# Two expert layers: first pass's rows by one-hot products, place table inside the loop, gate rows by ScalarE's queue, two blocks' residual adds on GpSimd

## The chip, the cores and the metric

One core of a Trainium2 chip runs the whole program. The metric is the device time of one execution in microseconds (us). The engines are called PE (TensorE, the matrix products), DVE (VectorE), ACT (ScalarE), POOL (GpSimd) and SP (SyncE, which here only issues transfers).

## The reference, cut to what matters

Two layers run over 384 tokens of 1024 channels (128 context tokens, 256 latent tokens): a mixer (layer 0) or attention (layer 1), and after each a mixture of 32 experts:

```python
g_prob = softmax(x @ w_rg + b_rg)                 # 4 groups, the best one is taken
e_v, e_i = top_k(logits of that group's 8 experts, 2)
gate = softmax(e_v) * g_p                         # two experts and two gates per token
hid = silu(x @ w_g[e]) * (x @ w_u[e])             # 1024 -> 256
y = sum over the token's two experts of gate * (hid @ w_d[e])
x = x + m[5] * y                                  # m[5]: the layer's gate row (adaLN)
```

The next layer, or the end of the program, begins with an RMS norm of x. Everything is float32.

## The kernel before, in words

Tokens lie in three blocks of 128 partitions (`X`, `H`, `NB` = 3). The experts are paired (16 pairs). One **round** of the expert loop has 22 **passes**: the 6 heaviest pairs get two passes, the other 10 one; a pass takes up to 32 tokens of each expert of its pair (`SLOTS`). The number of rounds comes from the counts of tokens at run time. With these inputs it is one round in each layer, 44 passes in all.

Ahead of the loop (`experts(l)`, one function for each engine) the **routing** is computed: PE multiplies the normed rows by the router's weights, DVE picks the experts, PE counts tokens in front of each (L988), and DVE turns the counts into a slot (`slot_p`) and a place (`slot_c`, which pass) for each of a token's two experts. From these DVE builds one-hot operands, and PE sums them into tables: four columns first (L999, the rows of passes 0 to 3, turned into row numbers on DVE, L1843 to L1846), and then a table for all rounds at once (L1005, 2 x 136 columns, operands L1848 to L1850, results L1864 to L1869).

In a **pass** POOL fetches the pass's 64 rows from DRAM by an indirect transfer (`gather`, L622 the row numbers, L625 the transfer); PE turns them (`turn_rows`, L1013), ACT copies the turned rows to SBUF (`x_copy`, L1392), PE multiplies by the gate and up weights (L1058), ACT applies Silu (L1404), DVE multiplies (`HID`, L1913), PE turns (L1070) and multiplies by the down weights (L1080). ACT and DVE split the result in two parts (L1411, L1923), and in the next pass PE spreads them over the tokens by a one-hot product (`combine`, L1024); DVE adds that to the sums (`add_half`, L1886). The transfers of rows for passes 0 and 1 are issued before the loop, and each later one when PE has turned the rows two passes earlier.

The expert weights come by SP's queue: 2 MB for each of gate, up and down of a pair (L453), into a ring of six slots, so that two pairs are in SBUF. Six transfers are issued as the slots come free ahead of the loop; in the loop a pair's gate and up slots are loaded again when its last gate and up product is done (ACT counts `gate_up_used`), its down slot when its last down product is.

Also ahead of the loop of layer 0, PE computes rows of the modulation for later layers from weights that stand in those ring slots. The last of them is called `places`: products (L751), a sum (L767 to L769), ACT's copy (L1242, L1243), POOL's product with the gain (L571) and its store to DRAM (`mod_rows`, L561). SP loads the sixth expert chunk only when that store has landed. POOL's queue then loads the layer's gate rows (1 MB) and in layer 0 the next norm's shift and scale rows (2 MB, both L525) from `mod_rows`.

After the loop DVE does the **end**: it adds the last sums, multiplies by the gate rows (`update_block`, L1939), adds to `X` (L1940), and norms the block (`norm_block`; ACT gives the squares and the root): block 0, then 1, then 2. After layer 1 that norm (L1517) is the result, and POOL's queue stores it (L679).

## Time and profile before

| | |
|---|---|
| time, median of 3 runs | 1055.38 us (1053.33 to 1055.83) |
| the profiled execution: its time, its span | 1052.37 us, 1050.5 us |
| busy: PE, DVE, ACT, POOL | 878.1, 520.7, 206.9, 123.2 us |
| mean granted clock of PE | 0.91 of 2.4 GHz |
| moved by DMA | 304.67 MB, mean 290 GB/s |

Rows of a timeline give start and length in us, the engine, the line of the kernel, the operation and its tiles, and in brackets how long the engine had been idle and what ended that. "SPq" is a transfer issued by SP. Two full levels of PE's clock occur: 1.00 (2.4 GHz) and 0.50 (1.2 GHz).

### The profile page before, as it was taken

The numbers are of one execution on the slowest core, as the hardware profiler recorded it, in microseconds if no ns is written. First come the engines' busy times: TensorE is split into PE (matmuls) and PEld (weight loads), VectorE is DVE, ScalarE is ACT, GpSimd is POOL, SyncE is SP. The second block draws the span as 40 slices with busy tenths as digits, with TensorE's granted clock in tenths as the row PEclk, the third lists the DMA queues.
The fourth block names the chain that finished last, engine by engine and source line by source line (L and its number), as shares of the span: only waits on it lengthen the run. The fifth ranks groups of instructions, "written<-read, shape, count | busy, mean of one in ns | idle before, by whom it ended". The sixth has DMA issues, their size and how long they took to land.

```text
span 1050.5 us, 17780 instructions
## 1 busy us (share of the span) xinstructions
PE 878.1 (84%) x6776; PEld 475.1 (45%) x6776; DVE 520.7 (50%) x1257; ACT 206.9 (20%) x428; POOL 123.2 (12%) x196
## 2 busy tenths in 40 slices
PE   2799999999799899786687997899589979886850
PEld 0455454645355455443333465445455545443420
DVE  1257532244656555452445464524656646454354
ACT  2223141212111111110122115212011111111021
POOL 2300011300321010010001000020211101000000
PEclk9899999898899999898888999999599989898875
DMA  9992440938899999999998523021699999999921
GB/s 306 366 333 80 144 176 15 395 128 301 330 365 407 417 416 417 413 413 418 416 387 330 180 81 130 1 86 44 255 366 391 417 412 418 418 415 419 417 117 60
DMA packets 78198, 304.67 MB, mean 290 GB/s; under 512 B 11512, under 2 KB 11824, under 8 KB 52648
## 3 DMA queue, kind: packets, MB, share of 16 engines
q1 hardware_dynamic: 66072, 277.08, 66.9%
q0 software_dynamic: 10768, 21.78, 5.9%
q10 hardware_dynamic: 1280, 4.72, 1.1%
q8 instruction: 55, 0.90, 0.4%
q14 instruction: 23, 0.19, 0.0%
HBM read 317.10 MB, written 5.32 MB: 307 GB/s over the span
## 4 chain that ended last, share of the span: by engine, by line
PE 67%; DMA 13%; DVE 7%; issue 5%; SPq 3%; ACT 3%; DVEq 0%; POOL 0%; ACTq 0%
PE psum L727 16%; PE psum L1058 15%; DMA ring<-in_w_exp_up 9%; PE psum L1080 6%; PE psum L1024 5%; PE psum L799 4%; PE psum L925 4%; PE psum L1013 3%; PE psum L751 3%; DVE ht L1886 3%; SPq L448 2%; DMA ring<-in_w_in_odd 2%; DMA ring<-in_w_mod 2%; PE psum L973 1%; PE psum L1189 1%
## 5 line engine op out<-in xcount | busy, mean ns | idle before, releaser
L1058 PE MATMUL psum<-ring,arena 128*32 128x256 f32 x2816 | 193.6, 436 | 60.6 <-issue 41.7
L1886 DVE TENSOR_TENSOR ht<-ht,psum 128x512 f32<-128x512 f32 x276 | 172.8, 679 | 34.0 <-PE psum L1024 34.0
L1058 PEld LDWEIGHTS psum<-ring,arena 128*32 128x32 f32 x2816 | 107.1, 125 | 159.5 <-issue 100.7
L727 PE MATMUL psum<-ring,ht 128*128 128x512 f32 (+1 forms) x432 | 170.3, 551 | 3.4 <-ACT ht L1257 2.7
L727 PEld LDWEIGHTS psum<-ring,ht 128*128 128x128 f32 x432 | 81.4, 191 | 85.7 <-issue 77.1
L1024 PE MATMUL psum<-y_top,to_token 64*128 64x512 f32 x276 | 88.0, 468 | 14.5 <-DVE y_low L1923 4.0
L1913 DVE TENSOR_TENSOR arena<-arena,psum 64x256 f32<-64x256 f32 x44 | 18.1, 412 | 164.5 <-ACT arena L1404 164.5
L1080 PE MATMUL psum<-ring,arena 128*32 128x512 f32 x704 | 84.7, 598 | 0.0
L1024 PE MATMUL psum<-y_low,to_token 64*128 64x512 f32 x276 | 71.3, 417 | 0.0
L751 PE MATMUL psum<-ring,cond_silu 128*32 128x512 f32 x384 | 50.8, 669 | 21.1 <-DMA ring<-in_w_mod 21.1
L1411 ACT ACTIVATE y_top<-psum,arena 128x512 fp32r<-128x512 f32 x44 | 30.2, 687 | 181.6 <-PE psum L1080 181.6
L1404 ACT ACTIVATE arena<-psum 64x256 f32<-64x256 f32 x44 | 16.7, 380 | 217.0 <-PE psum L1058 217.0
L622 POOL CAST arena<-arena 128x1 uint32 (+1 forms) x48 | 10.1, 211 | 390.8 <-PE psum L1013 369.8
L1013 PEld LDWEIGHTS psum<-ident,arena 32*128 32x128 f32 x736 | 44.0, 197 | 22.9 <-issue 22.9
L625 POOL DMA_INDIRECT arena<-h_rows,arena x48 | 48.7, 1016 | 42.9 <-POOL arena L622 40.4
L1024 PEld LDWEIGHTS psum<-y_top,to_token 64*128 64x128 f32 x276 | 34.5, 185 | 41.9 <-DVE ht L1886 32.3
L1923 DVE SCALAR_TENSOR_TENSOR y_low<-psum,arena,y_top 128x512 fp32r<-128x512 f32 x44 | 33.0, 750 | 40.0 <-ACT y_top L1411 40.0
L1013 PE MATMUL psum<-ident,arena 32*128 32x32 f32 x736 | 49.1, 272 | 3.9 <-issue 3.9
L561 POOL DMA_DIRECT2D mod_rows<-ring x20 | 10.7, 539 | 285.1 <-ACT ring L1245 283.9
L799 PE MATMUL psum<-ht,ring 128*128 128x384 f32 x128 | 43.6, 497 | 0.0
L925 PE MATMUL psum<-ring,ht 128*128 128x512 f32 x96 | 42.4, 598 | 0.0
L1392 ACT COPY arena<-psum 128x512 f32<-128x512 f32 x46 | 27.0, 587 | 56.1 <-PE psum L1013 56.1
(329 smaller groups left out, 914.3 us busy)
## 6 DMA issues: line engine op xcount, KB each, us to landing
ring<-in_w_exp_gate SPq DMA_DIRECT2D x32, 2048.0 KB, 15.6
ring<-in_w_exp_up SPq DMA_DIRECT2D x32, 2048.0 KB, 20.8
ring<-in_w_exp_down SPq DMA_DIRECT2D x32, 2048.0 KB, 20.8
ring<-in_w_mod SPq DMA_DIRECT2D x24, 2048.0 KB, 17.2
ring<-in_w_in_even SPq DMA_DIRECT2D x5, 2048.0 KB, 19.7
shift_scale<-mod_rows POOLq DMA_DIRECT2D x3, 2048.0 KB, 10.7
ring<-in_w_in_odd SPq DMA_DIRECT2D x3, 2048.0 KB, 19.7
ring<-in_w_out_even SPq DMA_DIRECT2D x2, 2048.0 KB, 8.3
```

The costliest lines, as they stand in the source:

```text
L625: pool.indirect_dma_start(XS[v], None, h_rows[l], bass.IndirectOffsetOnAxis(ap=from_row[v][:, 0:1].bitcast(U32), axis=0), bounds_check=T - ...
L727: mm = pe.matmul(psum[:, to, 0:cols], HT[:, b, k, :], w[:, k, :], start=(k == 0), stop=(k == KC - 1))
L751: mm = pe.matmul(psum[32 * j:32 * j + 32, to, :], cond_silu[:, k, 2 - 2 * half:34 - 2 * half], w[:, k, :], start=(half == 0 and r == 0), s ...
L799: mm = pe.matmul(psum[:, to, 0:T], w[:, k, c * P:(c + 1) * P], HT[:, :, k, :], start=(k == 0), stop=(k == KC - 1))
L925: mm = pe.matmul(bank(OUT_BANKS[0][c]), HT[:, b, k, :], w[n][:, k, :], start=(k == 4), stop=(k == 3))
L1013: t = pe.transpose(psum[:, n, SLOTS * k:SLOTS * (k + 1)], XS[v][side, k:D:KC], ident[side, side])
L1024: mm = pe.matmul(bank(BACK_BANKS[2 * b + n]), to_token[v][side, b * P:(b + 1) * P], rows[side, :], start=(part == 0), stop=(part == 1))
L1058: mm = pe.matmul(psum[to:to + SLOTS, 2, 0:256], XT[:, e, k, :], RG[:, 3 * u + a, e, k, :], start=(k == 0), stop=(k == KC - 1))
L1080: mm = pe.matmul(psum[to:to + SLOTS, 4, :], HTS[v][:, k, SLOTS * e:SLOTS * (e + 1)], RD[:, 3 * u + 2, e, k, n * 512:(n + 1) * 512], start= ...
L1411: act.activation(Y_HI, bank(4), ACT.Copy, scale=token[v][:, 1:2]).then_inc(M("y_top"), 1)
L1886: dve.tensor_tensor(acc, acc, bank(BACK_BANKS[c]), ALU.add).then_inc(M("added"), 1)
L1923: dve.scalar_tensor_tensor(Y_LO, bank(4), token[v][:, 1:2], Y_HI, ALU.mult, ALU.subtract).then_inc(M("y_low"), 1)
```

## The change

1. **First pass's rows by products** (`first_rows`). DVE builds `first_hot`, which says for each token whether and in which slot it is in pass 0; PE multiplies the normed rows, which are still in `H`, by it: 24 products of 128x128 by 64 columns, which give pass 0's turned rows directly. The transfer of pass 0's rows and its `turn_rows` go. The small table has two columns (passes 1 and 2) instead of four; it stands between the two halves of the 24.
2. **The table inside the loop.** It has 25 columns for one round instead of 136 for six (`PLACES`). PE makes it in pass 0 after the gate and up products, DVE turns it into row numbers after `HID` of pass 0 (`table`), and only then may PE go on with that pass's `combine`. At the end of a round DVE lowers `slot_c` by 22 and builds the operands for the next one. POOL's loop is written out in 22 passes with fixed columns. The gates of the tokens and the number of rounds are computed earlier on DVE.
3. **Gate rows by ScalarE's queue.** ACT issues the loads of gate rows (and in layer 0 of shift and scale rows) ahead of the loop, after waiting for the last `mod_rows` store (`rest_stored`).
4. **Residual adds on GpSimd.** For blocks 1 and 2 DVE adds the sums and multiplies by the gate rows in PSUM (`gated_sum`), and POOL adds to `X`. Block 1's part comes before block 0's norm.

On PE ahead of layer 0's loop stood (L999 the small table, L767 to L769 the sum of `places`, L1005 the large table, L1013 the turn of pass 0's rows):

```order
L999 MATMUL psum<-arena 128x4 [waits routing_sb]
L999 MATMUL psum<-arena 128x4 x5
L767 MATMUL psum<-mod_bias,pick_bias 4x512 [waits rest_row_ready,mod_part_sb]
L768 MATMUL psum<-ring,pick 4x512
L769 MATMUL psum<-mod_bias,pick_bias 4x512
L1005 MATMUL psum<-arena 128x272 [waits routing_sb]
L1005 MATMUL psum<-arena 128x272 x5
L1013 MATMUL psum<-ident,arena 128x32 [waits rest_row_ready,moe0_gathered_0]
L1013 MATMUL psum<-ident,arena 128x32 x15
```

and now (L1002 is `first_rows`, L1010 the small table):

```order
L1002 MATMUL psum<-arena,h 128x64 [waits routing_sb,rest_row_ready]
L1002 MATMUL psum<-arena,h 128x64 x11
L1010 MATMUL psum<-arena 128x2 [waits routing_sb]
L1010 MATMUL psum<-arena 128x2 x5
L1002 MATMUL psum<-arena,h 128x64 x12
L766 MATMUL psum<-mod_bias,pick_bias 4x512 [waits rest_row_ready,mod_part_sb]
L767 MATMUL psum<-ring,pick 4x512
L768 MATMUL psum<-mod_bias,pick_bias 4x512
```

The wait for pass 0's rows (`moe0_gathered_0`) is gone, and the large table, now 128x50, follows the gate and up products of pass 0.

On ACT in the same place stood (L1235 to L1243 the copies of `places`, L1392 `x_copy`, L424 the number of rounds, after which the loop begins):

```order
L1235 COPY ring<-psum 128x512 [waits mod_part_ps]
L1242 COPY ring<-psum 4x512 [waits mod_sum_ps]
L1243 ACTIVATE ring<-psum 4x512
L1392 COPY arena<-psum 128x512 [waits moe0_x_ps]
L424 TENSOR_LOAD arena [waits rounds_ready]
```

and now:

```order
L1247 COPY ring<-psum 128x512 [waits mod_part_ps]
L1432 COPY arena<-psum 128x512 [waits moe0_x_ps]
L1254 COPY ring<-psum 4x512 [waits mod_sum_ps]
L1255 ACTIVATE ring<-psum 4x512
L1404 DMA gate_rows<-mod_rows 128x2048 [waits rest_stored]
L1404 DMA shift_scale<-mod_rows 128x4096
L426 TENSOR_LOAD arena [waits rounds_ready]
```

Between `x_copy` and the loop ACT now waits for the store of the `places` rows.

On DVE at the end of layer 1 stood, from block 0's gate rows on:

```order
L1939 TENSOR_TENSOR arena<-ht,gate_rows 128x512 [waits moe1_added]
L1940 TENSOR_TENSOR x<-x,arena 128x512 [waits dve_links]
L1939 TENSOR_TENSOR arena<-ht,gate_rows 128x512
L1940 TENSOR_TENSOR x<-x,arena 128x512 [waits dve_links]
L1884 REGISTER_ALU
L1886 TENSOR_TENSOR ht<-ht,psum 128x512 [waits moe1_back_ps]
L1884 REGISTER_ALU
L1886 TENSOR_TENSOR ht<-ht,psum 128x512 [waits moe1_back_ps]
L1501 SCALAR_TENSOR_TENSOR small<-small 128x1 [waits squares]
```

and now:

```order
L1984 TENSOR_TENSOR x<-x,arena 128x512 [waits dve_links]
L1991 REGISTER_ALU
L1992 TENSOR_TENSOR psum<-ht,psum 128x512 [waits moe1_back_ps]
L1994 TENSOR_TENSOR arena<-psum,gate_rows 128x512 [waits x_updated,dve_links]
L1991 REGISTER_ALU
L1992 TENSOR_TENSOR psum<-ht,psum 128x512 [waits moe1_back_ps]
L1994 TENSOR_TENSOR arena<-psum,gate_rows 128x512 [waits x_updated,dve_links]
L1526 SCALAR_TENSOR_TENSOR small<-small 128x1 [waits squares]
```

Block 1's two gate products come ahead of block 0's norm, and its additions to `X` are POOL's.

The diff's core:

```diff
-PLACES = MAX_ROUNDS * PASSES + 4
+PLACES = PASSES + 3
...
             # POOL
-                for q in range(2):
-                    gather(q, q, static=True)
+                for q in range(1, 3):
+                    gather(q, one(first_row[:, q - 1:q]), q % 2)
...
-                for v in range(2):
-                    one_pass(v, v, static=True)
-                load_rows(u, (2, 3), gt_t[:, :], "gate_in")
-                if l == 0:
-                    load_rows(2, (0, 2), gs_t[:, :], "rows_in")
-                pool.wait_ge(S("table_ready"), 2 * l + 2)
                 R = rounds_of(pool, l)
-                with pool.Fori(1, R * (PASSES // 2)) as i:
-                    for v in range(2):
-                        one_pass(i * 2 + v, v)
+                with pool.Fori(0, R) as r:
+                    pool.wait_ge(M("table"), r + 1)
+                    for p in range(PASSES):
+                        q = r * PASSES + p
+                        pool.wait_ge(M("x_ps"), q + 2)
+                        gather(q + 3, tab[:, 1:2, p + 3:p + 4], (p + 1) % 2)
...
+                for c in range(2, 6):
+                    b, n = divmod(c, 2)
+                    pool.wait_ge(M("added"), last * 6 + (13 + c))
+                    pool.tensor_tensor(X[:, b, cols], X[:, b, cols], UPD_M[n], ALU.add).then_inc(S("x_updated"), 1)
...
             # PE
+                def first_rows(some):
+                    for k in some:
+                        for b in range(NB):
+                            mm = pe.matmul(psum[:, X_BANKS[0], 2 * SLOTS * k:2 * SLOTS * (k + 1)], H[:, b, k:D:KC], first_hot[:, b, :],
+                                           start=(b == 0), stop=(b == NB - 1))
...
+                    if p == 0:
+                        pe.wait_ge(M("in_table"), r * 7 + 1)
+                        for i in range(6):
+                            mm = pe.matmul(psum[:, 7, 0:2 * PLACES], in_slot[:, i, :], in_pair[:, i], start=(i == 0), stop=(i == 5))
+                        mm.then_inc(M("table_ps"), 1)
                     turn_rows(q + 1, 1 - v)
                     if p == 0:
-                        pe.wait_ge(S("table_ready"), 2 * l + 2)
+                        pe.wait_ge(M("table"), r + 1)
...
             # ACT
-                x_copy(0)
+                act.wait_ge(M("x_ps"), 1)
+                act.copy(XT, bank(X_BANKS[0]).rearrange("p (k e s) -> p e k s", e=2, k=KC)).then_inc(M("x_sb"), 1)
+                last_stored = mods("places")[0] if l == 0 else mods("norm_3")[0]
+                if l == 0:
+                    mod_row_copy(last_stored)
+                act.wait_ge(S("rest_stored"), 32 * (last_stored - FRONT + 1))
+                load_rows(u, (2, 3), gt_t[:, :], "moe_gate_in")
+                if l == 0:
+                    load_rows(2, (0, 2), gs_t[:, :], "rows_2_in")
...
             # DVE
+                link(dve.tensor_tensor(in_first, across(3), along(slot_c, 3), ALU.is_equal))
+                link(dve.tensor_tensor(in_slot[:, :, 0:2 * SLOTS], across(2 * SLOTS), along(slot_p, 2 * SLOTS), ALU.is_equal))
+                link(dve.tensor_tensor(hot_6, in_slot[:, :, 0:2 * SLOTS], in_first[:, :, 0:1].broadcast_to([P, 6, 2 * SLOTS]), ALU.mult))
+                dve.tensor_tensor(first_hot, hot_6[:, 0:NB, :], hot_6[:, NB:6, :], ALU.add).then_inc(S("routing_sb"), 1)
...
                     dve.tensor_tensor(HID[v], SGM[v], psum[0:2 * SLOTS, 2, 0:256], ALU.mult).then_inc(M("hidden"), 1)
+                    if p == 0:
+                        table(r)
...
+                    again(r, 4, dve.tensor_scalar(slot_c, slot_c, float(-PASSES), None, ALU.add))
+                    operands(lambda ins: again(r, 5, ins), lambda ins: again(r, 6, ins))
...
+                def gated_sum(b):
+                    for n in range(2):
+                        link(dve.tensor_tensor(found, ACC[:, b, cols], found, ALU.add))
+                        dve.wait_ge(S("x_updated"), 2 * NB * u + c - 1)
+                        dve.tensor_tensor(UPD_M[n], found, GT[:, 1, cols], ALU.mult).then_inc(M("added"), 1)
...
                 add_half(last, 0)
                 add_half(last, 1)
-                update_block(0)
-                add_half(last, 2)
-                add_half(last, 3)
+                update_first()
+                gated_sum(1)
                 norm_block(u + 1, 0)
-                add_half(last, 4)
-                add_half(last, 5)
-                for b in (1, 2):
-                    update_block(b)
-                    norm_block(u + 1, b)
+                gated_sum(2)
+                norm_block(u + 1, 1)
+                norm_block(u + 1, 2)
```

## Rows read from the trace of the kernel before

**Rows 1.** Windows of the two loops: engines' busy us, PE clock, DMA share, GB/s.

```profile
306.00:530.00 224.00, 189.92 (x2182) 105.63 (x2174) 113.86 (x275) 32.47 (x59) 22.67 (x38) 0.92 1.01 414
784.00:1000.00 216.00, 184.79 (x2110) 101.21 (x2109) 114.09 (x273) 32.11 (x58) 23.30 (x39) 0.92 1.01 413
```

**Rows 2.** The chain that ended last: start, length, what; late in either loop.

```profile
535.15 21.01 DMA ring<-in_w_in_odd
...
963.60 24.11 DMA ring<-in_w_exp_up
```

**Rows 3.** Windows at the loops' starts, columns as in the first.

```profile
286.00:302.00 16.00, 15.40 (x178) 8.44 (x178) 7.50 (x22) 3.06 (x5) 3.64 (x6) 0.81 0.74 274
...
288.00:289.00 1.00, 1.00 (x16) 0.56 (x12) 0.86 (x5) 0.00 (x0) 0.18 (x1) 0.50 0.00 0
...
780.00:785.00 5.00, 4.77 (x58) 3.04 (x50) 2.64 (x8) 0.97 (x2) 1.22 (x2) 1.00 0.58 165
```

**Rows 4.** Timeline of layer 0 from the small table to the loop's first load.

```profile
269.83 1.50 PE L999 MATMUL psum<-arena 128*128 128x4 f32 x12
...
273.78 0.22 DVE L1846 SCALAR_TENSOR_TENSOR arena<-arena,small 128x4 f32<-128x4 f32 x1
273.92 1.00 DVE L1848 TENSOR_TENSOR arena<-iota,arena 128x816 f32<-128x816 f32 x1
...
274.20 0.76 POOL L622 CAST arena<-arena 128x1 uint32<-128x1 f32 x1 [5.70 <-DMA mod_rows<-ring]
...
275.92 1.07 POOL L625 DMA_INDIRECT arena<-h_rows,arena  x1 [0.96 <-POOL arena L622]
...
277.06 5.38 PE L1005 MATMUL psum<-arena 128*128 128x272 f32 x12 [4.14 <-DVE arena L1850]
...
284.41 1.09 PE L1013 MATMUL psum<-ident,arena 32*128 32x32 f32 x16 [1.97 <-issue]
...
286.36 6.47 PE L1058 MATMUL psum<-ring,arena 128*32 128x256 f32 x64 [0.86 <-ACT arena L1392]
286.51 1.28 ACT L1404 ACT_TABLE_LOAD   x1 [0.39 <-issue]
...
288.28 0.37 SPq L453 DMA_DIRECT2D ring<-in_w_exp_down  x1
288.45 0.18 POOL L622 CAST arena<-arena 128x1 uint32<-128x1 f32 x1 [3.98 <-DMA mod_rows<-ring]
...
292.89 0.38 ACT L1404 ACTIVATE arena<-psum 64x256 f32<-64x256 f32 x1 [5.10 <-PE psum L1058]
...
293.75 0.50 PE L1024 MATMUL psum<-y_top,to_token 64*128 64x512 f32 x2
...
296.52 1.92 PE L1080 MATMUL psum<-ring,arena 128*32 128x512 f32 x16
...
302.26 0.39 SPq L453 DMA_DIRECT2D ring<-in_w_exp_gate  x1
```

**Rows 5.** Timeline of layer 1, the same stretch.

```profile
749.11 2.72 PE L999 MATMUL psum<-arena 128*128 128x4 f32 x12 [3.20 <-DVE arena L1797]
...
767.23 4.99 PE L1058 MATMUL psum<-ring,arena 128*32 128x256 f32 x64 [0.75 <-ACT arena L1392]
...
775.91 1.93 PE L1080 MATMUL psum<-ring,arena 128*32 128x512 f32 x16
...
781.65 0.38 SPq L453 DMA_DIRECT2D ring<-in_w_exp_gate  x1
```

**Rows 6.** Timeline of the program's end, DVE.

```profile
1016.27 1.28 DVE L1886 TENSOR_TENSOR ht<-ht,psum 128x512 f32<-128x512 f32 x2 [1.28 <-PE psum L1024]
...
1033.79 0.69 DVE L1940 TENSOR_TENSOR x<-x,arena 128x512 f32<-128x512 f32 x1
...
1035.27 0.16 DVE L1501 SCALAR_TENSOR_TENSOR small<-small 128x1 f32<-128x1 f32 x1 [0.79 <-ACT h L1224]
...
1036.48 1.29 DVE L1517 SCALAR_TENSOR_TENSOR h<-x,small,shift_scale 128x1024 f32<-128x1024 f32 x1
```

**Rows 7.** Groups by line: POOL's large two-input operation (busy us, mean ns | idle).

```profile
L580 POOL TENSOR_TENSOR arena<-arena,shift_scale 128x1536 f32<-128x1536 f32 x1 | 3.4, 3425 | 1.2 <-DMA mod_rows<-ring 1.2
```

More of the change, by code:

```diff
@@ L91, in shape_constants @@
         "k_before": (i[:, None] < i[None, :]).astype(np.float32),
-        "k_iota": np.broadcast_to(np.arange(PLACES, dtype=np.float32), (P, PLACES)).copy(),
+        "k_iota": np.broadcast_to(np.arange(P, dtype=np.float32), (P, P)).copy(),
         "k_masks": masks,
@@ L119 @@
 FRONT = len(MOD_GROUPS["front"])
-MOD_BANKS = {"even": (4, 4), "gate": (0, 1), "scale": (2, 3), "norm_1": (5, 3), "router": (2, 3), "places": (2, 3), "norm_2": (2, 7),
+MOD_BANKS = {"even": (4, 4), "gate": (0, 1), "scale": (2, 3), "norm_1": (5, 3), "router": (2, 3), "places": (4, 3), "norm_2": (2, 7),
              "attention": (2, 3), "norm_3": (0, 1)}
@@ L612, in experts, with gather @@
                     store_rest("router")
-                def column(q):
-                    return tab[:, 1:2, bass.ds(q, 1)]
                 def one(v):
                     return v.rearrange("p (f o) -> p f o", o=1)
-                def gather(q, v, static=False):
-                    row = one(first_row[:, q:q + 1]) if static else column(q)
+                def gather(q, row, v):
                     pool.tensor_copy(one(from_row[v][:, 0:1].bitcast(U32)), row).then_inc(M("row_looked_up"), 1)
@@ L674, in _ @@
             experts(1)
-            load(GS[:, 0, 0, :], d["final_norm_g"].rearrange("(o n) -> o n", o=1).broadcast_to([P, D]), "rows_in")
             for b in range(NB):
@@ L1051, in one_pass @@
                     pe.wait_ge(M("hidden"), q + 2)
-                    if l == 0 and p == 0:
-                        pe.wait_ge(S("rest_row_ready"), mods("places")[0] - FRONT + 1)
                     for k in range(KC):
@@ L1386, in experts, with load_rows @@
                     mod_copies(mods("router"))
-                    mod_copies(mods("places"))
+                    mod_part_copy(mods("places")[0])
+                def load_rows(n, part, dst, sem):
+                    src = mod_rows[n // 2, 3 * (n % 2) + part[0]:3 * (n % 2) + part[1]].rearrange("a s n -> (a s n)")
+                    act.dma_start(dst, src.rearrange("(o n) -> o n", o=1).broadcast_to([P, dst.shape[1]])).then_inc(S(sem), 16)
                 def x_copy(q):
@@ L1868, in experts, with again, operands @@
-                dve.tensor_tensor(tab[:, 0, :], tab[:, 1, :], tab_tmp, ALU.add)
-                dve.scalar_tensor_tensor(tab[:, 1, :], tab[:, 1, :], unused, tab_tmp, ALU.max, ALU.add).then_inc(S("table_ready"), 1)
+                def again(r, k, ins):
+                    ins.then_inc(M("in_table"), 1)
+                    dve.wait_ge(M("in_table"), r * 7 + (1 + k))
+                def operands(first, second):
+                    first(dve.tensor_tensor(in_pair[:, :, 0, :], across(PLACES), along(slot_c, PLACES), ALU.is_equal))
+                    second(dve.tensor_tensor(in_pair[:, :, 1, :], in_pair[:, :, 0, :], along(gates.rearrange("p j b -> p (j b)"), PLACES), ALU.mult))
+                    dve.tensor_tensor(in_pair[:, :, 0, :], in_pair[:, :, 0, :], along(dest, PLACES), ALU.mult).then_inc(M("in_table"), 1)
@@ L1871, in experts @@
+                operands(link, link)
                 dve.tensor_scalar(turn, rank, 2.0, -1.0, ALU.mult, ALU.add)
@@ L1909, in one_pass @@
                     v = p % 2
-                    lookup(q, v)
+                    if p > 0:
+                        lookup(q, p, v)
                     dve.wait_ge(M("gated"), q + 1)
```

156 lines of the change are left out of this document (83 added, 73 removed).

## The prediction

> **What bounds the kernel now.** I read the windows of the two expert loops first. In both the DMA share is 1.01 at about 414 GB/s [rows 1], so the transfers of weights are saturated from the first load inside the loop to nearly its end. PE has 34 of 224 us idle there [rows 1]. The chain of waits says the same from the other side: its long links are a chunk of weights that comes 21 us late at the end of layer 0 and 24 us late in layer 1 [rows 2]. A loop's length is thus the bytes it still has to move. Starting PE sooner is worth something only where it lets transfers start sooner and fill a stretch in which the DMA engines were not full.
>
> Such stretches stand at the loops' starts [rows 3]. In layer 0, from 286 to 302, the share is 0.74: 0.26 x 16 = 4.2 us are empty (5.4 by GB/s, (414 - 274) / 414 x 16), and from 288 to 289 nothing moves at all, because SP's sixth chunk waits until the `places` store has landed. In layer 1 the hole is 0.42 x 5 = 2.1 us (3.0 by GB/s). These are ceilings for all that the first three parts can gain. The stretch after layer 1 is different: 1016.27 to 1037.77, first sum added to last norm applied [rows 6], is a chain on DVE with no weights in it, and what is saved there shows in full.
>
> **Layer 0's start: about 0 (-1.6 to +2).** Added: 24 products of 64 columns. The bounds for one are L999's, 1.50 / 6 = 0.25 us at full clock and 2.72 / 6 = 0.45 at half [rows 4, 5] (x12 are six products of two records each), and L1005's 5.38 / 6 = 0.90 with 272 columns at half clock [rows 4]. I take 0.25 here, as L999's own products in this place run at it: 24 x 0.25 + 1.5 = 7.5 us from about 269.8. Pass 0's turned rows are ready near 277.3, with the copy under 279; before, L1058 began at 286.36 after the large table (5.38), a 1.97 us wait for the transferred rows and the turn (1.09) [rows 4]. So pass 0's gate and up products can begin some 7 us sooner. That doesn't reach the down products, for three reasons.
>
> (a) The small table now ends behind twelve of the 24 products, about 1.2 us later than before, net of its smaller operands. POOL's two row transfers, its clearing of `HT` and the `places` store follow in its queue, so all come later by that, less at most 0.6 which POOL's CAST gets back: it took 0.76 beside DVE's L1848 and 0.18 elsewhere [rows 4], and L1848 has moved away. The store, which had landed when SP's load went out at 288.28, lands at 288.9 to 289.4.
>
> (b) ACT now waits for that store ahead of its loop, with pass 0's Silu and all its later work queued behind. From 289.4: two issues at 0.37 (SPq's row), the 0.39 idle, the table load 1.28, the Silu 0.38: 292.2 [rows 4], against 292.89 + 0.38 = 293.27. The cover that ACT loses is small because Silu came late before as well.
>
> (c) DVE then makes `HID` (about 0.4, as the Silu) and six table steps at 0.22 (L1846's row) = 1.3, and PE may combine at 293.9; before, it did at 293.75. L1080 follows 2.77 later (296.52 - 293.75) [rows 4], at 296.7. That is even.
>
> The first load inside the loop (before at 302.26) depends on the gate and up products of pass 1, which stand behind L1080. Their speed is the open price: PE will have waited several microseconds ahead of `combine`. After the 1.97 us wait of the trace the clock stood at 0.50 through 288 to 289 [rows 3], and L1058 took 6.47 us there where 4.99 is what layer 1 shows [rows 4, 5]. I bound this at 0 and 3 us. It is partly given back, since the 3 MB of gate, shift and scale rows go out earlier, at about 290, into the hole; but moving them there only moves the hole unless the loop's loads start sooner as well. One transfer of rows fewer is 0.25 MB, 0.6 us at 414 GB/s. I take 0, between -1.6 and +2.
>
> **Layer 1's start: -1.2 (-2.3 to +1.7).** Here no `places` store is left and ACT doesn't wait. The small table ran at half clock [rows 5]. 24 x 0.45 + 2.7 = 13.5 us from about 749.7 gives 763.2, the copy 0.8, so the gate and up products begin near 764.0 instead of 767.23. Given back: the table products ahead of the turn, between L999's 1.5 and 2.7 us, and DVE's table of which 0.2 to 1.2 isn't covered. L1080, before at 775.91, comes 1.5 sooner to 0.7 later, and 0.7 sooner at my middle. With the gather less (0.6) I take -1.2. The ceiling is the hole, 2.1 us; the other end is a half clock held through the table and the turn, +1.7.
>
> **End of layer 0: 0.** The residual adds are quicker there too, but layer 1 begins with a weight chunk that is already 21 us late [rows 2]; DVE's saving is hidden by it. POOL's adds delay the `norm_2` store behind them on POOL's queue, by an estimated 7 us; the load that waits for it is a chunk that is not the next one due. If that cover went, up to 3 us would show; I leave it in the range.
>
> **End of layer 1: -3.0 (-1.8 to -4.3).** DVE loses four additions to `X` at 0.69: 2.8 us [rows 6]. Blocks 1 and 2 are summed before block 0's and 1's norm, so ACT's squares for block 2 run beside block 1's norm, and the 0.79 that DVE waited for them ahead of L1501 [rows 6] goes, with its start about 0.9. Together 3.7, and 3.9 with what the shorter operands and waits between the adds leave (two gaps of 0.1, an estimate). POOL's price isn't shown for 512 columns. Its large two-input operation took 3425 ns for 1536 columns [rows 7], a third is 1.14, and I take 1.25 with its start; the lower bound is DVE's 0.69, the upper 3.4, the row as it stands. Four adds at 1.25 are 5.0, in pairs beside some 8 us of DVE's work, so they keep up; at 3.4 POOL would be the bound and the gain about nil. The row nearest in shape decides for 1.25. The three new operand steps at the loop's end (L1848's 1.00 with 816 elements [rows 4], with 150 about 0.4 each) fall in the 1.28 us that DVE waited for PE's last sums [rows 6]; at most 0.3 sticks out.
>
> One thing speaks against this part. The POOL CAST of 0.76 ended together with DVE's L1848, an operation with two SBUF inputs (273.92 + 1.00 and 274.20 + 0.76) [rows 4]. If POOL's adds hold DVE's like operations in turn, the norm's small steps and its apply (L1517, 1.29 [rows 6]) stand still while an add runs: I put this at 0.75 once and 0.15 once, so 3.9 becomes 3.0. The gated sums read one operand from PSUM and are not exposed in this way.
>
> By the Trainium skill (SBUF - State Buffer, "Who interferes with whom") a DVE instruction with two SBUF inputs contends with a GpSimd instruction that reads SBUF, and whichever starts first keeps the shared ports for its whole length. The row of 0.76 agrees; by that rule alone the end gives -3.0, without it -3.9.
>
> **The sum.** 0 - 1.2 + 0 - 3.0 = -4.2. The profiled execution took 1052.4, 3.0 below the median of the runs shown. So 1048.2 on its scale, and **1051.2** against the median of 1055.4.
>
> **The rivals.** 0.3% (3.2 us) is about what a measurement of this kernel can tell from no change.
> 1. My forecast, within 1049.5 to 1053: 0.47.
> 2. *The earlier starts show in full.* PE keeps its full clock and the loads inside both loops begin sooner: layer 0 -1.6, layer 1 -2.1, end -3.5, together -7.2: 1048.2. For it speaks the empty 4.2 and 2.1 us [rows 3]; against it that Silu, the table and the down products still stand in line. 0.22.
> 3. *The starts lose what the end gains.* A cold PE costs +2 in layer 0, layer 1 gives nothing, POOL's adds hold DVE so that the end gives -2 to -3: 1054.4 to 1055.4, no change. This is also the time if the change doesn't do what it says: with one round in each layer, a table for each round saves no round. 0.23.
> 4. *ACT's wait takes the place of PE's.* The `places` store goes out behind two row transfers and shares the DMA engines with SP's chunks. Issued at about 284.5 it had landed in under 3.98 us [rows 4]; the row transfer issued at 275.92 had PE wait until 284.41, 8.5 us [rows 4]. If the store takes 8.5, it lands at 293.5 to 294, Silu ends at 296.8, and everything from the down products on is 4.7 late; with a cold PE, +3, that is +7.7 - 4.2 = +3.5: 1058.9, slower. It decides from a landing at about 296.8 on if PE stays warm (7.4 late, which is 4.2 and 3.2), from 293.8 if not. Against it: in the trace SP's queue is empty while that store travels (0 GB/s, [rows 3]). 0.08.
>
> **The range.** 1046.5 (rival 2 with the end at -4.3 and something from layer 0) to 1056.0 (rival 3 with 0.6 for a layer-0 end that shows). Faster by over 0.3% means under 1052.2: most of cases 1 and 2, 0.62. Within: 0.30. Slower: 0.08, rival 4.
>
> **What would show it.** Right: the first load inside the loops at 302 to 305 and at about 781; Silu of pass 0 of layer 0 ending near 292; `first_rows` at 0.25 and 0.45 a product; from the first sum added to the last norm applied about 18.5 us instead of 21.5; POOL's adds near 1.25 each, and DVE's small norm steps longer than 0.2 beside them. Wrong: a load inside layer 0's loop before 300 or after 306, PE at 0.50 through pass 1, POOL's adds over 2 us, the DMA share in the loops under 1.

## The result, and the profile after

The change is slower: 1061.0 us (median of 10 runs, 1055.4 to 1063.7) against 1055.4 (10 runs, 1053.0 to 1057.2), a ratio of 1.0052 with a 95% interval of 1.0032 to 1.0071, or +5.5 us (+3.4 to +7.5). Measured once more beside other kernels it gave 1.0054 (1.0033 to 1.0076). The forecast was 1051.2 us, 4.2 under before, in a range up to 1056.0.

The profiled execution of the change is the fastest of its ten: 1055.35 us, span 1053.4, where before's was 1052.37 and 1050.5. One trace can't carry a few microseconds here, since stretches that nothing in the change touches differ from one execution to the next (before layer 0 this one is some 3 us ahead of before's, and in attention, with PE at half clock from 644 to 653, it loses some 2 us of that again). So stretches are compared from an event inside them: in layer 0 from the first of the 24 products (before: from L999, at 269.83 [rows 4]), in layer 1 from the counts of tokens ahead of them (L990, now L989). Of each timeline only the rows that the text reads are shown.

**Layer 0's start**, timeline of the change:

```profile
266.52 5.97 PE L1002 MATMUL psum<-arena,h 128*128 128x64 f32 x24
272.28 2.67 PE L1010 MATMUL psum<-arena 128*128 128x2 f32 x12
274.81 5.92 PE L1002 MATMUL psum<-arena,h 128*128 128x64 f32 x24
...
280.66 0.59 PE L766 MATMUL psum<-mod_bias,pick_bias 64*4 64x512 f32 x1
...
283.49 4.34 PE L1065 MATMUL psum<-ring,arena 128*32 128x256 f32 x64
...
284.75 1.27 POOL L573 TENSOR_TENSOR ring<-ring 4x512 f32<-4x512 f32 x1 [1.62 <-ACT ring L1255]
286.31 1.15 POOL L563 DMA_DIRECT2D mod_rows<-ring  x2 [0.29 <-POOL ring L573]
287.76 1.54 PE L1071 MATMUL psum<-arena 128*128 128x50 f32 x12
288.55 0.37 SPq L455 DMA_DIRECT2D ring<-in_w_exp_down  x1
288.56 0.40 ACTq L1404 DMA_DIRECT2D gate_rows<-mod_rows  x1
...
291.76 0.38 ACT L1421 ACTIVATE arena<-psum 64x256 f32<-64x256 f32 x1
...
293.34 0.24 DVE L1905 SCALAR_TENSOR_TENSOR arena<-arena,small 128x25 f32<-128x25 f32 x1
293.73 0.80 PE L1033 MATMUL psum<-y_top,to_token 64*128 64x512 f32 x2 [3.43 <-DVE arena L1905]
...
297.46 3.64 PE L1094 MATMUL psum<-ring,arena 128*32 128x512 f32 x16
300.88 4.18 PE L1065 MATMUL psum<-ring,arena 128*32 128x256 f32 x64
...
304.99 1.06 PE L1022 MATMUL psum<-ident,arena 32*128 32x32 f32 x16
...
305.43 0.39 SPq L455 DMA_DIRECT2D ring<-in_w_exp_gate  x1
```

Read it from the top. The 24 products are 5.97 + 5.92 = 11.9 us, 0.50 each, where 0.25 was forecast from [rows 4]; with the small table the piece is 14.2 us, not 7.5. The gate and up products begin at 283.49, 17.0 us after the first product; before, 16.5 (286.36 - 269.83). Of the 17.0, 14.2 are this piece and 2.8 the sum of `places` (L766 to L768), which now stands behind it and runs at half clock. So not one microsecond of the "7 us sooner" exists. Everything behind is late: POOL waits 1.62 us for ACT's copy of that sum before it can prepare the store, the store lands 22.0 us after the first product (before 18.5), ACT's two loads go out at the very moment it lands, Silu follows, DVE's last table step ends at 293.58, and PE has waited 3.43 us for it. `combine` comes 27.2 us after the first product, before 23.9: +3.3.

Then PE is slow. The down products L1094 take 3.64 us where L1080 took 1.92 [rows 4], and from `combine` to the loop's first load it is 11.7 us, before 8.5 (302.26 - 293.75): +3.2. Together the first load is 6.5 us late (5.5 in a second profiled execution of the change). Windows of the change, columns as in [rows 1], show PE's clock:

```profile
271.00:272.00 1.00, 1.00 (x6) 1.00 (x6) 0.00 (x0) 0.00 (x0) 0.00 (x0) 0.64 1.29 434
...
285.00:286.00 1.00, 1.00 (x24) 0.55 (x20) 0.00 (x0) 0.00 (x0) 1.00 (x1) 1.00 0.00 0
...
292.00:293.00 1.00, 0.00 (x0) 0.00 (x0) 0.78 (x4) 0.73 (x2) 0.00 (x0) 0.50 1.02 434
...
301.00:302.00 1.00, 1.00 (x16) 0.47 (x12) 0.11 (x1) 0.69 (x1) 0.00 (x0) 0.50 1.09 459
302.00:303.00 1.00, 1.00 (x24) 0.53 (x20) 0.96 (x4) 0.00 (x0) 0.00 (x0) 1.00 0.52 197
```

It falls to 0.50 at 271.3, during the 24 products, is at 1.00 again by 285, falls while PE waits for the table, and stands at 0.50 until 302, through `combine`, the down products and the next gate and up products. DMA engines stand empty at 285 to 286 meanwhile. None of it is given back: the next layer's first weight chunk (`in_w_in_odd`) is issued 271.6 us after the first product, before 265.3, and the mean rate of that stretch is 394 GB/s instead of 405.

**Layer 1's start,** first two rows of before, then the change:

```profile
744.59 1.33 PE L990 MATMUL psum<-arena,ones 128*128 128x96 f32 x6
...
773.14 0.50 PE L1024 MATMUL psum<-y_top,to_token 64*128 64x512 f32 x2
```

```profile
749.76 1.33 PE L989 MATMUL psum<-arena,ones 128*128 128x96 f32 x6
...
754.86 5.99 PE L1002 MATMUL psum<-arena,h 128*128 128x64 f32 x24 [3.78 <-DVE arena L1831]
...
769.84 5.21 PE L1065 MATMUL psum<-ring,arena 128*32 128x256 f32 x64 [0.75 <-ACT arena L1432]
...
777.88 0.50 PE L1033 MATMUL psum<-y_top,to_token 64*128 64x512 f32 x2 [0.36 <-DVE arena L1905]
...
781.12 2.97 PE L1094 MATMUL psum<-ring,arena 128*32 128x512 f32 x16
...
787.91 0.38 SPq L455 DMA_DIRECT2D ring<-in_w_exp_gate  x1
```

The gate and up products do begin 2.6 us sooner (20.1 us after the counts against 22.6), `combine` is 0.4 sooner, and the first load 1.1 later (38.2 against 37.1), because from `combine` to it there are now 10.0 us, before 8.5.

**The end**, timeline, and POOL's group of the change:

```profile
1023.01 1.28 DVE L1924 TENSOR_TENSOR ht<-ht,psum 128x512 f32<-128x512 f32 x2 [0.53 <-PE psum L1033]
...
1028.50 2.58 POOL L654 TENSOR_TENSOR x<-x,arena 128x512 f32<-128x512 f32 x2 [8.87 <-DVE arena L1994]
...
1030.27 0.82 DVE L1518 SCALAR_TENSOR_TENSOR small<-small 128x1 f32<-128x1 f32 x1
...
1036.00 0.83 DVE L1518 SCALAR_TENSOR_TENSOR small<-small 128x1 f32<-128x1 f32 x1
...
1039.07 0.16 DVE L1518 SCALAR_TENSOR_TENSOR small<-small 128x1 f32<-128x1 f32 x1
...
1039.65 1.28 DVE L1545 SCALAR_TENSOR_TENSOR h<-x,small,shift_scale 128x1024 f32<-128x1024 f32 x1
```

```profile
L654 POOL TENSOR_TENSOR x<-x,arena 128x512 f32<-128x512 f32 x8 | 10.1, 1267 | 32.4 <-DVE arena L1994 32.1
```

From the first sum added to the last norm applied it is 17.9 us (1023.01 to 1040.93), before 21.5 [rows 6]: -3.6. POOL's add takes 1.27 us. The small step L1518 takes 0.82 and 0.83 beside POOL's adds of blocks 1 and 2 and ends with them (1030.27 + 0.82, 1028.50 + 2.58); without an add it takes 0.16.

### The profile page after: what moved, and what is told of

Its sections match the earlier page's. It is cut to its first block, busy times and chain, and to the rows that moved or that the text cites. A ratio compares the mean times of both kernels' runs of the same rounds, so it can differ in the third digit from the quotient of the medians.

```text
span 1053.4 us, 17779 instructions
## 1 busy us (share of the span) xinstructions
PE 894.4 (85%) x6840; PEld 491.6 (47%) x6840; DVE 518.2 (49%) x1263; ACT 206.8 (20%) x428; POOL 130.2 (12%) x201
## 4 chain that ended last, share of the span: by engine, by line
PE 68%; DMA 14%; issue 5%; DVE 5%; SPq 3%; ACT 2%; DVEq 0%; POOL 0%; ACTq 0%
PE psum L726 16%; PE psum L1065 14%; DMA ring<-in_w_exp_up 9%; PE psum L1094 6%; PE psum L1033 5%; PE psum L798 4%; PE psum L924 4%; PE psum L750 3%; PE psum L1022 3%; SPq L450 2%; DVE ht L1924 2%; PE psum L1002 2%; DMA ring<-in_w_in_odd 2%; DMA ring<-in_w_mod 2%; DMA ring<-in_w_exp_gate 1%
## 5 line engine op out<-in xcount | busy, mean ns | idle before, releaser
L1065 PE MATMUL psum<-ring,arena 128*32 128x256 f32 x2816 | 188.3, 427 | 60.8 <-issue 40.5
L1924 DVE TENSOR_TENSOR ht<-ht,psum 128x512 f32<-128x512 f32 x268 | 167.7, 680 | 33.7 <-PE psum L1033 33.7
L1065 PEld LDWEIGHTS psum<-ring,arena 128*32 128x32 f32 x2816 | 104.5, 123 | 158.9 <-issue 96.1
L1094 PE MATMUL psum<-ring,arena 128*32 128x512 f32 x704 | 88.7, 623 | 0.0
L750 PE MATMUL psum<-ring,cond_silu 128*32 128x512 f32 x384 | 50.2, 664 | 20.9 <-DMA ring<-in_w_mod 20.9
L620 POOL CAST arena<-arena 128x1 uint32<-128x1 f32 x48 | 9.1, 189 | 429.0 <-PE psum L1022 389.7
L623 POOL DMA_INDIRECT arena<-h_rows,arena x48 | 48.7, 1014 | 41.5 <-POOL arena L620 40.3
L1022 PE MATMUL psum<-ident,arena 32*128 32x32 f32 x704 | 46.9, 272 | 0.0
L1094 PEld LDWEIGHTS psum<-ring,arena 128*32 128x32 f32 x704 | 18.9, 112 | 45.4 <-issue 45.4
## 6 DMA issues: line engine op xcount, KB each, us to landing
ring<-in_w_exp_gate SPq DMA_DIRECT2D x32, 2048.0 KB, 16.5
ring<-in_w_in_odd SPq DMA_DIRECT2D x3, 2048.0 KB, 20.1
```

Source lines behind the costliest of these rows:

```text
L623: pool.indirect_dma_start(XS[v], None, h_rows[l], bass.IndirectOffsetOnAxis(ap=from_row[v][:, 0:1].bitcast(U32), axis=0), bounds_check=T - ...
L750: mm = pe.matmul(psum[32 * j:32 * j + 32, to, :], cond_silu[:, k, 2 - 2 * half:34 - 2 * half], w[:, k, :], start=(half == 0 and r == 0), s ...
L1022: t = pe.transpose(psum[:, n, SLOTS * k:SLOTS * (k + 1)], XS[v][side, k:D:KC], ident[side, side])
L1065: mm = pe.matmul(psum[to:to + SLOTS, 2, 0:256], XT[:, e, k, :], RG[:, 3 * u + a, e, k, :], start=(k == 0), stop=(k == KC - 1))
L1094: mm = pe.matmul(psum[to:to + SLOTS, 4, :], HTS[v][:, k, SLOTS * e:SLOTS * (e + 1)], RD[:, 3 * u + 2, e, k, n * 512:(n + 1) * 512], start= ...
L1924: dve.tensor_tensor(acc, acc, bank(BACK_BANKS[c]), ALU.add).then_inc(M("added"), 1)
```

## The experiments

Three theories of the loss stood against each other. A: the 24 products cost 0.50 us because their stationary operand is read in steps of eight elements, and what stands behind them is late by that. B: ACT's wait for the store, with Silu behind it, is what costs. C: the table's place inside the loop costs, by the wait for DVE and by what it leaves PE's clock at. That the end (part 4) gains in any case was tried apart. Times in the table are the starts of these rows in us from the first product (layer 0) or the counts (layer 1), each from one trace. "First load" is the first weight chunk that is issued inside the loop, "odd chunk" the next layer's first one. In "the change, again" the changed kernel was run beside e5 to e7.

| kernel | ratio to before (95%) | Silu | `combine` | first load | `combine` to load | odd chunk | layer 1: `combine` to load, load |
|---|---|---|---|---|---|---|---|
| before | 1 | 23.1 | 23.9 | 32.4 | 8.5 | 265.3 | 8.5, 37.1 |
| the change | 1.0052 | 25.2 | 27.2 | 38.9 | 11.7 | 271.6 | 10.0, 38.2 |
| the change, again | 1.0054 (1.0033-1.0076) | 25.3 | 27.2 | 38.0 | 10.8 | 270.8 | 10.1, 38.6 |
| e1 end only | 0.9944 (0.9923-0.9964) | 22.9 | 23.8 | 32.3 | 8.5 | 264.8 | 8.5, 38.0 |
| e9 end only, again | 0.9975 (0.9956-0.9994) | 22.8 | 23.6 | 32.1 | 8.5 | 264.8 | 8.5, 37.2 |
| e2 `places` first | 1.0027 (1.0006-1.0047) | 20.9 | 26.4 | 37.0 | 10.6 | 269.4 | 10.9, 40.3 |
| e3 loads by POOL | 1.0015 (0.9991-1.0039) | 21.9 | 24.6 | 36.1 | 11.5 | 268.8 | 10.1, 38.3 |
| e4 neighbouring channels | 1.0003 (0.9982-1.0025) | 23.6 | 25.5 | 36.5 | 11.0 | 269.7 | 8.5, 36.4 |
| e5 table ahead | 0.9998 (0.9976-1.0020) | 26.2 | 27.0 | 35.5 | 8.5 | 268.1 | 8.5, 37.1 |
| e6 table ahead, POOL | 0.9998 (0.9974-1.0022) | 24.6 | 25.5 | 34.0 | 8.5 | 268.3 | 8.5, 37.3 |
| e10 table ahead, SP | 0.9998 (0.9974-1.0022) | 24.9 | 25.8 | 34.3 | 8.5 | 267.7 | 8.5, 36.3 |
| e7 permuted, e6 | 0.9952 (0.9933-0.9971) | 18.4 | 18.9 | 27.4 | 8.5 | 268.1 | 8.5, 35.2 |
| e11 permuted, e10 | 0.9916 (0.9887-0.9945) | 20.0 | 20.5 | 29.0 | 8.5 | 263.4 | 8.5, 34.9 |

**Part 4 alone** (`gated_sum`, `update_first` and POOL's adds put into the kernel before), run twice.

> The kernel before with part 4 of the change alone (sums of blocks 1 and 2 gated in PSUM, their additions to X on POOL). If the loss sits at the loops' starts, this alone is faster than before by 2.5 to 4 us (in the trace of the change the stretch from the first sum added to the last norm applied went from 21.5 to 17.9 us), ratio about 0.997, and its loops begin as before's do. If POOL's additions also cost something in layer 0's end or the norm_2 store that they push back is waited for, the gain is under 1.5 us.

> The kernel before with part 4 alone once more, for a second interval: its first gave 0.9944 (0.9923 to 0.9964) where its trace shows 3.6 us gained at the end, 0.9966. If the end is all there is, ratios near 0.996 to 0.997 belong in the interval; if something in the rest of the program gains as well, it stays under 0.995.

The intervals of the ratios, 0.9944 and 0.9975, overlap at 0.9956 to 0.9964, which is 3.8 to 4.6 us. The trace has 17.9 us for the end in both, as in the change, so 3.6 of it is shown; more than that isn't. Part 4 gains, and the starts of the loops stand as before's.

**The `places` sum ahead of the products' bulk** (theories A and C).

```diff
+                first_rows(range(0, 1))
+                if l == 0:
+                    mod_sum(mods("places")[0])
-                first_rows(range(0, 4))
+                first_rows(range(1, 4))
...
                 pool.sem_inc(M("row_looked_up"), 1)
+                if l == 0:
+                    store_rest("places")
```

> The changed kernel with the sum of the places rows after the first three of the 24 products instead of behind all of them, ACT's copies of it ahead of the copy of pass 0's rows, and its store ahead of the two row transfers on POOL. Theory A (the 24 products cost 0.50 us each, 14.5 us with the small table, and all that stands behind them, the store, ACT's loads, Silu, the table, is late by that): the store lands before 278, SP's sixth chunk leaves 10 us sooner, Silu of pass 0 follows its products at once (about 289 instead of 291.8), PE combines near 291 instead of 293.7 and stays warm, the first load in layer 0's loop comes 4 to 6 us sooner: 1055 to 1057 where the change has 1061. Theory C (the table inside the loop is what PE waits for, whatever the store does): PE still combines within 1 us of 293.7 and the time stays at 1060 to 1061.

The store and the sixth chunk come 10 us sooner and Silu 4.3, but `combine` only 0.8. A new wait took over: the row transfers of passes 1 and 2 now stand behind the store on POOL's queue, are issued at 282.95 and 285.13 behind the sixth chunk of weights, and PE waits for them.

```profile
281.77 0.37 SPq L455 DMA_DIRECT2D ring<-in_w_exp_down  x1
282.95 1.09 POOL L623 DMA_INDIRECT arena<-h_rows,arena  x1 [0.96 <-POOL arena L620]
...
295.18 1.09 PE L1023 MATMUL psum<-ident,arena 32*128 32x32 f32 x16 [3.07 <-DMA arena<-h_rows,arena]
```

It tells little of A against C, and the ratio's interval overlaps the change's. It shows that a store can also come too early for what stands behind it.

**Loads back on POOL's queue** (theory B).

```diff
-                act.wait_ge(S("rest_stored"), 32 * (last_stored - FRONT + 1))
-                load_rows(u, (2, 3), gt_t[:, :], "moe_gate_in")
...
                     store_rest("places")
+                load_rows(u, (2, 3), gt_t[:, :], "moe_gate_in")
```

> The changed kernel with the loads of gate, shift and scale rows back on POOL's queue, issued when the places store has landed; ACT waits for no store. Theory B (the loss in layer 0 is ACT's wait for the store with Silu behind it): Silu at about 288.5 instead of 291.8, PE combines near 291, the first load in the loop 4 to 6 us sooner, 1055 to 1057. Theory A gives nearly the same here in layer 0, since the wait is gone however late the store is; layer 1 is unchanged under both. Theory C: no change, 1060 to 1061. If PE's half clock and not the wait is what costs, the combine moves by 3 us and the first load in the loop by no more.

Silu 3.4 us sooner, `combine` 2.6 sooner, the first load 1.9 to 2.8 sooner. So ACT's wait is real and is part of it, but PE is as slow after `combine` (11.5) though it waits only 0.36 us there instead of 3.43; so the first load gains no more than `combine` did, as the last sentence of the expectation has it. B is not enough, and the ratio's interval overlaps the change's.

**Neighbouring channels** (theory A).

```diff
-  H[:, b, k:D:KC], first_hot[:, b, :],
+  H[:, b, k * P:(k + 1) * P], first_hot[:, b, :],
```

> The changed kernel with the stationary operand of the 24 products taken as 128 neighbouring channels of the normed rows instead of every eighth one: pass 0's experts are given the channels in another order, so pass 0's results are of other data; work and sizes are the same. Theory A with its cause in the operand's step of 8 elements: a product takes about 0.25 us at full clock and 0.45 at half instead of 0.50, in layer 0 the rows and the small table take 8 to 11 us instead of 14.2, pass 0's rows and the places store are 3 to 6 us sooner, and the time is 3 to 6 us under the change's 1061. If the step of the operand is not the cause, a product stays at 0.50 in both layers and the time at 1061.

```profile
270.25 2.89 PE L1002 MATMUL psum<-arena,h 128*128 128x64 f32 x24
272.98 1.45 PE L1010 MATMUL psum<-arena 128*128 128x2 f32 x12
274.29 4.51 PE L1002 MATMUL psum<-arena,h 128*128 128x64 f32 x24
...
284.37 1.14 POOL L563 DMA_DIRECT2D mod_rows<-ring  x2 [0.29 <-POOL ring L573]
...
290.60 0.37 SPq L455 DMA_DIRECT2D ring<-in_w_exp_down  x1
...
293.82 0.38 ACT L1421 ACTIVATE arena<-psum 64x256 f32<-64x256 f32 x1
...
754.75 5.36 PE L1002 MATMUL psum<-arena,h 128*128 128x64 f32 x24 [3.78 <-DVE arena L1831]
...
777.49 0.50 PE L1033 MATMUL psum<-y_top,to_token 64*128 64x512 f32 x2 [0.36 <-DVE arena L1905]
...
786.00 0.38 SPq L455 DMA_DIRECT2D ring<-in_w_exp_gate  x1
```

The kernel leaves out the matching order of channels in the experts' weights, so pass 0's results are of other data; the passes are as many. The first twelve products take 2.89 us, 0.24 each; in layer 1, at half clock, twelve take 5.36, 0.45 each. That the step of eight is the price is shown: 0.50 against 0.24 and 0.45. The piece shrinks from 14.2 to 8.5 us. But the store, issued at 284.4 to 285.5, lands only at 290.6, behind SP's two chunks, which fill the DMA engines (over 400 GB/s) until 287; in the change it was issued at 286.3 into empty ones and landed 1.1 us after the second issue. So ACT's wait eats 4 of the 5.7 us of layer 0. The ratio falls from 1.0052 to 1.0003 all the same, some 5 us, of which the trace shows 1.1 to 1.9 at the odd chunk and about 2 at layer 1's first load.

**The table ahead of the loop again** (theory C; made once, for one round).

```diff
-                    if p == 0:
-                        pe.wait_ge(M("in_table"), r * 7 + 1)
...
+                pe.wait_ge(M("in_table"), 1)
+                for i in range(6):
+                    mm = pe.matmul(psum[:, 7, 0:2 * PLACES], in_slot[:, i, :], in_pair[:, i], start=(i == 0), stop=(i == 5))
...
-                    if p == 0:
-                        table(r)
...
+                table(0)
                 dve.wait_ge(S("rows_cleared"), 7 * (l + 1))
```

> The changed kernel with the table's six products and DVE's six steps ahead of the loop again (made once, right for the one round that these inputs need), still 25 columns wide; ACT still waits for the places store. Theory C (the table's place between pass 0's gate and up products and its combine is what costs): PE combines at about 24 to 28 us after the places products began instead of 30.8, stays at full clock, the stretch from combine to the first load in layer 0's loop is 8.5 us as before the change instead of 11.7, in layer 1 8.5 instead of 10.0, and the time is 3 to 6 us under the change's. Theory A (the price of the 24 products, then ACT's wait): combine moves by the 1.4 us of DVE's steps at most, PE is as cold as in the change, time within 2 us of the change's.

```profile
283.46 2.80 PE L1101 MATMUL psum<-arena 128*128 128x50 f32 x12
286.18 6.37 PE L1065 MATMUL psum<-ring,arena 128*32 128x256 f32 x64
...
293.48 0.50 PE L1033 MATMUL psum<-y_top,to_token 64*128 64x512 f32 x2
...
301.98 0.39 SPq L455 DMA_DIRECT2D ring<-in_w_exp_gate  x1
```

`combine` comes no sooner (27.0), yet the first load does by 2.5 to 3.4 us: `combine` runs at 0.50 us a pair of records instead of 0.80, and the stretch behind it is 8.5 us in both layers, as before the change. 1.0054, measured beside it, becomes 0.9998, about 5.9 us. C holds in layer 0, in a form that its expectation had only half: what the table's place costs there is the clock under which pass 0's second half runs, not a later `combine`. In layer 1 it takes more than the table's place: e4 has the table inside the loop too, waits the same 0.36 us for it, and is at 8.5 there as well. Why PE's clock fell at 779.9 us in the change and not in e4 is open.

**Both** (table ahead, loads by POOL), and **the loads by SP's queue** instead, behind the sixth chunk.

> The kernel of the run before with the loads of gate, shift and scale rows on POOL's queue as well, so that neither ACT's wait nor the table in the loop is left and of the starts only the 24 products at 0.50 us remain. Theory A and C together: the first load in layer 0's loop comes within 1 us of the kernel before's 36.0 us after the places products began (the change has 42.5), with the end's 3.6 us gained the time is 1 to 5 us under before. If this is not under before, the 24 products alone cost what the end gains.

> The changed kernel with the table ahead of the loop and the loads of gate, shift and scale rows on SP's queue, behind the sixth chunk of weights, so that neither ACT nor the row transfers on POOL's queue stand behind them. Against the same with POOL's queue (first load in layer 0's loop 33.95 us after the first of the 24 products, ratio 0.9998): the start is the same, and if row transfers behind the 3 MB on POOL's queue cost nothing there, the ratio stays within 0.998 to 1.001.

The first load is 1.5 to 1.8 us later than before's rather than within 1, and the odd chunk 2.3 to 3.0 later; with the end's 3.6 the sum is nearly nothing, and the ratio is 0.9998 in both. The answer to e6's last sentence is yes: with ACT's wait and the table's place both gone, the 24 products at 0.50 us cost about what the end gains. The parts of the loss don't add up one by one, since one hides behind another: e6, without ACT's wait as well, is no faster than e5.

**Permuted channels**: the norm writes its rows in the order in which the products read neighbours.

```diff
-  t = pe.transpose(psum[:, n, SLOTS * k:SLOTS * (k + 1)], XS[v][side, k:D:KC], ident[side, side])
+  t = pe.transpose(psum[:, n, SLOTS * k:SLOTS * (k + 1)], XS[v][side, k * P:(k + 1) * P], ident[side, side])
...
-  link(dve.scalar_tensor_tensor(H[:, b, cols], X[:, b, cols], root, GS[:, 1, s, cols], ALU.mult, ALU.mult))
+  def every_eighth(v):
+      return v.rearrange("p (c k) -> p k c", k=KC)[:, 4 * n:4 * n + 4, :] if u % 2 else v[:, cols]
...
+  link(dve.scalar_tensor_tensor(to, every_eighth(X[:, b, :]), root, every_eighth(GS[:, 1, s, :]), ALU.mult, ALU.mult))
...
-  d["w_router_group"][l].rearrange("(k p) n -> p k n", k=KC)
+  d["w_router_group"][l].rearrange("(p k) n -> p k n", k=KC)
```

> The kernel of the run before with the normed rows of the expert layers written in another order of channels (channel 8c+k at place 128k+c, the router's weights loaded to match), so that the 24 products and the turns read neighbouring channels; DVE's norm reads X and the rows in steps of 8 elements instead. Theory A: a product 0.24 us at full clock, the rows and the small table 8.5 us instead of 14.2, the first load in layer 0's loop 3 to 5 us sooner than in the run before, time under the kernel with only the end changed (about 0.994 of before) if the holes of the DMA close, equal to it if they don't. If DVE's reads in steps cost double, layer starts lose 2 us of it.

> The kernel with permuted channels, the table ahead of the loop and the loads on SP's queue. With POOL's queue PE waited 5.6 us for pass 3's rows at 306 us, whose transfer had been issued at 293.3 behind the 3 MB of gate, shift and scale rows on the same queue, and layer 0's loop gave back the 5 us that it had begun sooner. If that is the cause, the wait is gone here, the first load of layer 1's first weight chunk comes 2 to 4 us sooner after the first products than the 268 us of the run before, and the time falls to 0.989 to 0.993 of before, under the kernel with only the end changed. If the DMA's holes move elsewhere (PE sets the pace in the six heavy pairs), it stays at 0.995.

The first load stands at 27.4 us, 5 us before before's. With POOL's queue layer 0 gives it all back (odd chunk at 268.1):

```profile
290.61 0.58 POOL L527 DMA_DIRECT2D gate_rows<-mod_rows  x1 [4.93 <-DMA mod_rows<-ring]
291.19 0.54 POOL L527 DMA_DIRECT2D shift_scale<-mod_rows  x1
...
293.33 1.07 POOL L623 DMA_INDIRECT arena<-h_rows,arena  x1 [0.86 <-POOL arena L620]
...
311.97 1.06 PE L1025 MATMUL psum<-ident,arena 32*128 32x32 f32 x16 [5.61 <-DMA arena<-h_rows,arena]
```

Pass 3's rows, issued at 293.33 behind 3 MB on the same queue, hold PE up 5.6 us at 306. With SP's queue that wait is gone, the odd chunk is issued 263.4 us after the first product, 1.9 sooner than before and 4.7 sooner than in e7, and the ratio is 0.9916 (0.9887 to 0.9945), some 9 us under before: the best version here, as its expectation said (0.989 to 0.993). Of the 9 us the traces show 1.9 at the odd chunk, 2.2 at layer 1's first load and 3.6 at the end. It lies clear of the end alone as measured beside it (e9), though not of e1.

The order of channels also changes the turn of every pass, which reads neighbours too. From e11:

```profile
298.54 0.68 PE L1028 MATMUL psum<-ident,arena 32*128 32x32 f32 x16
```

That is 0.68 us where the change takes 1.06 (304.99). At the loops' starts one such turn stands ahead of `combine`, so some 0.4 of the gain there is the turn's and not the products'. What the order of channels would give to the kernel before, with its transferred rows, was not run; so that part 1 pays in e11 is likely but not shown. That the products' price counts in the time is shown by two pairs, the change against e4 (about 5 us) and e6 against e7 (0.9998 to 0.9952, about 5 us, with the turns).

## Why the prediction was wrong

**What bounds the kernel: right.** The loops are bound by DMA, and a start counts by what it does to the holes at the loops' beginnings. It cuts both ways: 6.5 us lost at the first load were 6.2 at the next layer's chunk.

**The 24 products: this step failed.** The text took L999's 0.25 us for a product. L999's stationary operand is contiguous; that of the new products is `H[:, b, k:D:KC]`, every eighth element, and this stands in the diff. They measured 0.50 at either clock, 14.2 us instead of 7.5 with the small table. The upper bound, L1005's 0.90, was named and then not used: it should have stayed in the range, for 24 x (0.90 - 0.25) is 15.6 us. The Trainium skill (SBUF - State Buffer, under "Door 1: The DMA port swizzle") says that consecutive accesses run at full rate only within a line of 16 bytes, four elements of fp32, and pay for each new line. A step of eight elements meets a new line each time, so the runs agree in kind (0.50 against 0.24 and 0.45); it is a rule that spoke against the change and that the prediction did not weigh.

**(a) to (c), "that is even": wrong by 3.3 us.** The chain was the right one: store, ACT's two issues, table load, Silu, `HID`, six steps, `combine`. The store landed 22.0 us after the first product instead of 19.1 to 19.6. Point (a) put POOL's queue 1.2 us later, less up to 0.6; the row numbers reached POOL 5.1 us later (9.4 after the first product, before 4.4), and the store then waited for PE's sum of `places` behind all 24 products, which (a) doesn't reckon with. Most of both comes of products twice as long. From landing to Silu's end it was 3.6 us, forecast 2.8. Rival 4's mechanism, ACT's wait in the place of PE's, is what happened; its cause was not a slow transfer (the DMA engines were empty) but a late issue. The argument against that rival was misread: it took 288 to 289 for the whole way of the store, while from 283 to 286, as it was issued, the trace of before shows the engines full:

```profile
284.00:285.00 1.00, 0.59 (x12) 0.62 (x12) 0.87 (x6) 0.00 (x0) 0.47 (x1) 1.00 1.10 451
```

**PE's clock after the wait: mis-sized.** It was bounded at 0 to 3 us and taken at nothing, on the ground that rows loaded sooner would pay it back. It measured 3.2 and 2.3 us in layer 0 (the change and its second trace), and 1.5 and 1.6 in layer 1, and nothing paid it back. e5 shows that in layer 0 it hangs on what stands between the gate and up products and `combine`: with the table ahead of the loop the same stretch is 8.5 us, at full clock.

**Layer 1: -1.2 forecast, +1.1 and +1.5 measured,** inside the range given there. The earlier start was right (2.6, forecast 3.2), and what was given back ahead of `combine` nearly (0.4 and 0.1 left, forecast 0.7; the middle of the forecast's own terms, 3.2 - 2.1 - 0.7, is 0.4). The 1.5 us of half clock behind it were the other end of the range. About 1 us of this first load is chance: e1, whose start is before's, has it at 38.0; but its stretch from `combine` on is 8.5.

**The ends: right.** Layer 0's shows no gain: from the odd chunk to layer 1's counts it is 209.4 us before, 208.3 to 211.9 in the others, without order. The `norm_2` store is issued 21.9 us after the odd chunk instead of 15.1, 6.8 later where 7 was estimated, and the cover held: the second chunk behind it goes out after 41.6 us, before 41.7 (`in_w_out_odd`). Layer 1's measured -3.6, forecast -3.0. POOL's add is 1.27 us, forecast 1.25. The hold of POOL on DVE is there, at 0.66 us twice (0.82 against 0.16), 1.3 instead of 0.9. The gain without it was then 4.9 instead of 3.9: the wait of 0.79 stood ahead of two blocks' norms and went twice, and a wait of 1.04 for ACT in block 0's norm became 0.27. That the total came so near is in part luck, as two terms were too small in opposite ways. By the Trainium skill (SBUF - State Buffer, "Who interferes with whom") a DVE instruction with two inputs from SBUF contends with a GpSimd instruction that reads SBUF; the rows of 0.82 and 0.83 agree.

**The sum.** In the traces: layer 0 +5.5 to +6.2, layer 1 +1.1 to +1.5, the end -3.6: +3.0 to +4.1, against +5.5 (3.4 to 7.5) measured. Forecast: 0, -1.2, -3.0. Of the 9.7 us between forecast and result layer 0 has about 6 and layer 1 about 2.5, the end takes 0.6 back, and some 2 are not assigned. Rival 3 had the right mechanisms (a cold PE, starts that lose what the end gains) but priced layer 0's start at +2; rival 4 had the time (1058.9) by a transfer that was not slow.

## What to carry to other kernels

Price a new product by a row whose operands have the same steps, not only the same shape: here the step of the stationary operand doubled it, and a different order of channels (e11) took it back. Where a chain of small dependent steps is moved into the gap between two full stretches of PE, count the clock of the stretch behind it as well as the wait. And before a bulk load changes its queue, look at which small transfers will stand behind it: the same 3 MB cost 4.7 us more on the queue of the row transfers than on that of the weights where the loop starts early (e7, e11), and 0.6 where it starts 5 to 7 us later (e6, e10).

## What was not expected of the hardware

- An fp32 product with a 128x128 stationary operand in steps of eight elements takes 0.50 us at either clock; contiguous 0.24 at 2.4 GHz and 0.45 at 1.2 GHz.
- PE's clock fell to 0.50 at 271.3 us while PE had no idle time, 4.8 us into those products; in the six other traces with them in steps of eight it fell in the same stretch.
- DVE's norm step with operands in steps of eight took 1.15 us (mean) for 128x512 in e11 where it took 0.75 contiguous, and the following add 1.09 against 0.69.
- The same small store landed 1.1 us after its last issue with the DMA engines empty and 5.1 us after it with two weight chunks under way (the change, e4).
